# Moving operands of the matmuls to one offset modulo 256 bytes, and the wide products in order of width

## The chip, the core and the metric

The kernel runs on one core of a Trainium2 chip. The metric is the device time of one execution in microseconds. The runs below give a median; beside them stands one profiled execution, whose trace all rows are from. PE is TensorE's matmul, PEld its weight load, DVE is VectorE, ACT ScalarE, POOL GpSimd, SP SyncE.

## The reference

Two blocks of a network over 256 positions of width 1024, one after the other. All weights are float32. Reduced to what the products look like:

```
x = x + even_mixer(rmsnorm(x))          # gated convolutions, then @ w_out
x = x + conv_glu_ffn(rmsnorm(x))        # (silu(conv(h @ w_gate)) * (h @ w_up)) @ w_down
x = x + odd_mixer(rmsnorm(x))           # linear recurrence and dilated attention
x = x + conv_glu_ffn(rmsnorm(x))
for l in (0, 1):                        # second block, each norm with shift and scale
    x = x + 0.5 * g1 * swiglu(h)        # D_FF = 2816
    x = x + g2 * (pool and latent attention)(h)
    x = x + 0.5 * g3 * swiglu(h)
return rms_norm(x)
```

So there are six feed-forward networks (FFN), each 1024 to 2816 (twice) and back to 1024. They hold most of the products.

## The kernel before

Everything is kept with the channel on the partitions: X is 8 tiles of 128 channels by 256 positions. A float32 product is made of three float32r products (the rounded part `h` and the rest `l` of each factor: wh·HH, wh·HL, wl·HH). Weights arrive in 253 units of up to 1024 KB, in a fixed order. For each unit SyncE loads it into one of three `raw` buffers, ScalarE copies it to `wh` (`hi`, L1041), VectorE writes `wl = raw - wh` (`lo`, L1479), and TensorE consumes both. Each of `raw`, `wh`, `wl` has three buffers; ScalarE waits for the end of the unit that last used the buffer (`w_used`), TensorE for `split_done`.

An FFN has 11 blocks of 256 hidden channels (NFB). The first two blocks' gate and up units are **raw units** (`raw_unit`, L635): they work on the rows XH, XL before the norm's factor is known; XH is a view of FX with rows of XROW = 288 floats, of which 258 are read where the norm has a shift, else 256. The other nine blocks have two **wide units** (`paired`, L678): for each of the 8 tiles k two products of `wh` with HP[:, k] (HH and HL side by side, 512 columns, L684) into two banks, and two of `wl` with HH[:, k] (256 columns, L687). Each block ends in a **down** unit (L763 to L778): 48 products of 256 columns (L772), whose moving operands are the gated inputs, FP[0] and FP[1] by turns (views of FX, which is free by then), F0 for the first block. The mixers' products are made by `product` (L665, its matmul on L674), with HP as the moving operand, or with FX in the latent attention's q projection, or with the weights moving and HP stationary where the result is wanted by position.

The tensors lie one after another in SBUF in the order of their declarations (L327 to L364). HP, FX, XL and F0 have their own tensors of SKEW = 28 floats (112 bytes), the data, and 4 floats. `raw`, `wh`, `wl`, `ada`, X before them are multiples of 256 bytes long, HP's tensor is 16512 bytes long, T, Z and WK are multiples of 256, FX's tensor is 9344, XL's 8320, F0's 4224.

VectorE and ScalarE also do the gate's arithmetic of each block (add PSUM to the parts kept, taps of the convolution in the two FFNs of the first block, silu, product, split into FP). In five of the FFNs VectorE sums up to four 128x1024 products per block for the modulation (`ada`, L1578). The order on each engine is the order in the program text.

Of the kernel before, what the change touches and what calls it, by code (L numbers as in the profile page):

```python
# [17 lines left out]
F32R = mybir.dt.float32r  # L18
# [6 lines left out]
P = 128  # L25
D = 1024
S = 256
KD = D // P
# [2 lines left out]
NFB = F // FB  # L31
EPS = 1e-6
RW = S + 2
XROW = 288
SKEW = 28
NB = S // P

# [279 lines left out]
def build(nc, A, const, out):  # L317

    ctx = ExitStack()
    with ctx:  # L320
        def sb(name, shape, dt=F32):
            return ctx.enter_context(nc.sbuf_tensor(name, shape, dt))
# [12 lines left out]
        T = sb("T", [P, KD, S])  # L335
        Z = sb("Z", [P, 6720])
        WK = sb("WK", [P, 4608])
        FX = sb("FX", [P, SKEW + KD * XROW + 4], F32R)[:, SKEW:SKEW + KD * XROW]
        XH = FX.rearrange("p (k s) -> p k s", s=XROW)[:, :, 0:RW]
        XL = sb("XL", [P, SKEW + KD * S + 4], F32R)[:, SKEW:SKEW + KD * S].rearrange("p (k s) -> p k s", s=S)  # L340
        FP = [FX[:, 4 * XROW:4 * XROW + 1024], FX[:, 0:1024]]
        FH = [f[:, 0:512].rearrange("p (k s) -> p k s", s=S) for f in FP]
        FL = [f[:, 512:1024].rearrange("p (k s) -> p k s", s=S) for f in FP]
        F0 = sb("F0", [P, SKEW + 1024 + 4], F32R)[:, SKEW:SKEW + 1024].rearrange("p (b k s) -> p b k s", k=2, s=S)
        TF = F0[:, 0], F0[:, 1]
        G0 = sb("G0", [P, KD])
        SH = sb("SH", [P, 6, KD, 2], F32R)
# [18 lines left out]
        def bank(i, a=0, n=512, rows=slice(0, P)):  # L366
            return PS[rows, i, a:a + n]
# [15 lines left out]
        def pairs(ap, w=S):  # L383
            return ap.rearrange("p (t s) -> p t s", s=w)
# [246 lines left out]
        def _(pe):  # L631
# [3 lines left out]
            def raw_unit(n, dst, shift, first=None, between=None, narrow=P):  # L635
# [20 lines left out]
                for part in parts:  # L656
                    for m in range(2):
                        for k in part:
                            if first and m == 0 and k % 2 == 0:
                                pe.wait_ge(lr_ready, v + k // 2 + 1)  # L660
                            last = mm(bank(dst + m, 0, S, slice(0, rows[m])), lhsT=w(0, k, m * P, rows[m]), rhs=XL[:, k, :],  # L661
                                      start=False, stop=k == KD - 1, skip_group_check=True)
# [15 lines left out]
            def paired(bk, lhs, k_tiles, whole=None):  # L678

                for k in range(k_tiles):  # L680
                    if whole and k % 2 == 0:
                        pe.wait_ge(h_ready, FILL[whole] + k // 2 + 1)
                    for m in range(2):
                        mm(pairs(bank(bk + m)), lhsT=lhs(0, k, m * P), rhs=HP[:, k], start=k == 0, stop=False,  # L684
                           skip_group_check=True)
                    for m in range(2):
                        last = mm(bank(bk + m, 0, S), lhsT=lhs(1, k, m * P), rhs=HH[:, k, :], start=False,  # L687
                                  stop=k == k_tiles - 1, skip_group_check=True)
                return last
# [65 lines left out]
            def ffn(f, name):  # L755
# [3 lines left out]
                def wide(n, bk, off=0, whole=None):  # L759
                    w = weights(n, KD, off)  # L760
                    paired(bk, lambda p, k, a: w(p, k, a, P), KD, whole=whole).then_inc(w_used, 1)
# [707 lines left out]
        def _(dve):  # L1469
# [20 lines left out]
            def raw_lo(name, c, gain):  # L1490
# [6 lines left out]
                for t in (2 * c, 2 * c + 1):  # L1497
                    last = stt(XL[:, t, :], X[:, t, :], gain(t), XH[:, t, 0:S].bitcast(F32), ALU.mult, ALU.subtract)  # L1498
                last.then_inc(lr_ready, 1)
# [653 lines left out]
```

## Time and profile before

| | us |
|---|---|
| median of 3 runs | 1557.11 (1554.96 to 1557.14) |
| the profiled execution's own time | 1556.0 |
| its span, first to last instruction | 1554.1 |
| PE busy | 1529.1 (98%) |
| VectorE busy | 1254.7 (81%) |
| ScalarE busy | 848.0 (55%) |

Busy time of an engine is the time in which at least one of its instructions is under way. Matmuls overlap each other, so the mean duration of one is its latency and not what it costs; the distance from one start to the next is. The mean granted clock of TensorE over the span is 0.997 of the full one.

### The profile page before, as it was taken

The numbers are of one execution on the slowest core, as the hardware profiler recorded it, in microseconds if no ns is written. First come the engines' busy times: TensorE is split into PE (matmuls) and PEld (weight loads), VectorE is DVE, ScalarE is ACT, GpSimd is POOL, SyncE is SP. The second block draws the span as 40 slices with busy tenths as digits, with TensorE's granted clock in tenths as the row PEclk, the third lists the DMA queues.
The fourth block names the chain that finished last, engine by engine and source line by source line (L and its number), as shares of the span: only waits on it lengthen the run. The fifth ranks groups of instructions, "written<-read, shape, count | busy, mean of one in ns | idle before, by whom it ended". The sixth has DMA issues, their size and how long they took to land.

```text
span 1554.1 us, 26739 instructions
## 1 busy us (share of the span) xinstructions
PE 1529.1 (98%) x10894; PEld 1420.1 (91%) x10894; DVE 1254.7 (81%) x1588; ACT 848.0 (55%) x1014; POOL 52.0 (3%) x61
## 2 busy tenths in 40 slices
PE   9989999999999999999999999999999999999998
PEld 7989999998799999999999999999999999999997
DVE  7978989787578998978878797887888888785555
ACT  6656555564466545744446664445644456664443
POOL 1001000000010000000000010000000000100000
PEclk9999999999999999999999999999999999999999
DMA  7505886544247875498863359886598844355551
GB/s 300 204 16 193 323 317 242 193 163 160 75 138 296 308 289 190 168 338 312 317 234 140 116 195 325 319 310 230 191 331 308 313 176 166 136 191 189 188 189 68
DMA packets 59805, 344.11 MB, mean 221 GB/s; under 512 B 6800, under 2 KB 7312, under 8 KB 28752
## 3 DMA queue, kind: packets, MB, share of 16 engines
q1 hardware_dynamic: 58752, 340.80, 61.4%
q0 software_dynamic: 544, 1.97, 0.3%
q8 instruction: 54, 0.88, 0.2%
q10 hardware_dynamic: 432, 0.27, 0.1%
q14 instruction: 23, 0.19, 0.0%
HBM read 341.96 MB, written 1.05 MB: 221 GB/s over the span
## 4 chain that ended last, share of the span: by engine, by line
PE 83%; DVE 11%; ACT 3%; issue 3%; DMA 1%; SPq 0%; ACTq 0%; DVEq 0%
PE PS L684 25%; PE PS L772 23%; PE PS L687 13%; PE PS L674 7%; PE PS L652 5%; PE PS L741 3%; DVE wl L1479 3%; PE PS L661 2%; DVE Z L1822 2%; DVE XL L1498 2%; PE PS L823 1%; DMA raw<-weights 1%; ACT wh L1041 1%; DVE RS L1511 1%; PE PS L848 1%
## 5 line engine op out<-in xcount | busy, mean ns | idle before, releaser
L1479 DVE TENSOR_TENSOR wl<-raw,wh 128x2048 fp32r<-128x2048 f32 (+2 forms) x256 | 569.8, 2229 | 126.3 <-ACT wh L1041 124.5
L1041 ACT ACTIVATE wh<-raw 128x2048 fp32r<-128x2048 f32 (+2 forms) x256 | 475.7, 1860 | 125.5 <-PE PS L772 103.9
L684 PE MATMUL PS<-HP,wh 128*128 128x512 f32 x1728 | 538.6, 393 | 0.0
L687 PEld LDWEIGHTS PS<-HP,wl 128*128 128x128 f32 x1728 | 324.0, 187 | 74.4
L687 PE MATMUL PS<-HP,wl 128*128 128x256 f32 x1728 | 344.0, 281 | 0.0
L772 PE MATMUL PS<-FX,wh 128*128 128x256 f32 x1920 | 306.7, 279 | 0.0
L684 PEld LDWEIGHTS PS<-HP,wh 128*128 128x128 f32 x1728 | 265.2, 189 | 0.0
L772 PEld LDWEIGHTS PS<-FX,wh 128*128 128x128 f32 x1920 | 262.5, 188 | 0.2
L772 PE MATMUL PS<-FX,wl 128*128 128x256 f32 x960 | 197.9, 279 | 0.0
L1578 DVE SCALAR_TENSOR_TENSOR ada<-ada,AR 128x1024 f32<-128x1024 f32 x144 | 172.9, 1219 | 0.0
L772 PEld LDWEIGHTS PS<-FX,wl 128*128 128x128 f32 x960 | 149.9, 188 | 0.0
L652 PE MATMUL PS<-FX,wh 128*128 128x258 f32 (+2 forms) x592 | 143.1, 284 | 6.8 <-ACT wh L1193 1.9
L652 PE MATMUL PS<-FX,wl 128*128 128x258 f32 (+2 forms) x592 | 141.7, 282 | 0.5 <-DVE wl L1740 0.5
L1105 ACT ACTIVATE WK<-PS 128x512 f32<-128x512 f32 x54 | 32.3, 598 | 179.7 <-PE PS L687 179.7
L674 PE MATMUL PS<-HP,wh 128*128 128x256 f32 x696 | 122.1, 279 | 1.7 <-ACT HP L1072 0.9
L652 PEld LDWEIGHTS PS<-FX,wh 128*128 128x128 f32 (+1 forms) x592 | 109.9, 187 | 9.9 <-ACT FX L1056 2.7
L674 PEld LDWEIGHTS PS<-HP,wh 128*128 128x128 f32 x696 | 105.2, 188 | 7.0 <-issue 4.1
L652 PEld LDWEIGHTS PS<-FX,wl 128*128 128x128 f32 (+1 forms) x592 | 110.4, 188 | 0.7 <-DVE wl L1740 0.7
L674 PE MATMUL PS<-HP,wl 128*128 128x256 f32 x348 | 94.9, 276 | 0.0
L1134 ACT ACTIVATE WK<-PS 128x512 f32<-128x512 f32 x54 | 32.0, 592 | 97.1 <-PE PS L687 97.1
L661 PE MATMUL PS<-XL,wh 128*128 128x256 f32 (+1 forms) x592 | 76.3, 281 | 0.0
L661 PEld LDWEIGHTS PS<-XL,wh 128*128 128x128 f32 (+1 forms) x592 | 71.9, 187 | 0.5
(272 smaller groups left out, 1664.8 us busy)
## 6 DMA issues: line engine op xcount, KB each, us to landing
raw<-weights SPq DMA_DIRECT2D x242, 1024.0 KB, 5.0
ada<-ada_w SPq DMA_DIRECT2D x144, 512.0 KB, 6.5
raw<-weights SPq DMA_DIRECT2D x6, 768.0 KB, 4.4
raw<-weights SPq DMA_DIRECT2D x4, 576.0 KB, 4.7
X<-x SPq DMA_DIRECT2D x2, 512.0 KB, 5.7
raw<-weights SPq DMA_DIRECT2D x2, 512.0 KB, 6.8
out<-Z SPq DMA_DIRECT2D x4, 256.0 KB, 2.3
AR<-c POOLq DMA_DIRECT2D x1, 512.0 KB, 7.1
```

Source lines behind the costliest of these rows:

```text
L652: mm(bank(dst + m, 0, width, slice(0, rows[m])), lhsT=w(a, k, m * P, rows[m]), rhs=XH[:, k, 0:width], start=k == 0 and a == 0, stop=False, ...
L661: last = mm(bank(dst + m, 0, S, slice(0, rows[m])), lhsT=w(0, k, m * P, rows[m]), rhs=XL[:, k, :], start=False, stop=k == KD - 1, skip_gro ...
L674: last = mm(dst, lhsT=lhs(a, k), rhs=rhs(b, k), start=first and i == 0, stop=first and i == len(order) - 1, skip_group_check=not first)
L684: mm(pairs(bank(bk + m)), lhsT=lhs(0, k, m * P), rhs=HP[:, k], start=k == 0, stop=False, skip_group_check=True)
L687: last = mm(bank(bk + m, 0, S), lhsT=lhs(1, k, m * P), rhs=HH[:, k, :], start=False, stop=k == k_tiles - 1, skip_group_check=True)
L741: last = mm(bank(bk, m * S, S), lhsT=w(a, k, m * P, P), rhs=H[b][:, k, :], start=m == 0 and k == 0 and i == 0, stop=False, skip_group_chec ...
L772: last = mm(bank(m // 2, (m % 2) * S, S), lhsT=w(a, k, m * P, P), rhs=rhs(b, k), start=begins and i == 0 and m % 2 == 0, stop=False, skip_ ...
L1041: last = A_(dst(wh), src, ACT.Copy)
L1105: A_(pairs(E), PS[:, 4:6, S:], ACT.Copy).then_inc(g_copy, 1)
L1134: A_(pairs(G), PS[:, 6:8, S:], ACT.Copy).then_inc(u_copy, 1)
L1479: last = tt(dst(wl), src, dst(wh).bitcast(F32), ALU.subtract)
L1578: stt(w, w, 1.0, AR[:], ALU.mult, ALU.mult, accum_out=AS[:, bass.ds(off * KD + step, 1)]).then_inc(ada_sum, 1)
```

## The change

All moving operands except HP go into one tensor MV, which starts where FX's tensor started, 32 + 28 floats ahead of its first data. Rows of FX get 320 floats (1280 bytes, five times 256) in place of 288 (1152 bytes, four and a half times), XL and F0 follow directly. The moving data of FX (each row), FP[0], FP[1], XL and F0 then start 112 bytes past a multiple of 256, as HP does. What lies behind (G0, SH, AR, PR, CN and the rest) moves by 896 bytes. In `paired` the loop over k is split in two: all sixteen products of 512 columns, then all sixteen of 256. The number and shapes of the instructions, the semaphores and the order of units are the same.

```diff
@@ -31,7 +31,7 @@
 NFB = F // FB
 EPS = 1e-6
 RW = S + 2
-XROW = 288
+XROW = 320
 SKEW = 28
 NB = S // P
 
@@ -335,13 +335,14 @@
         T = sb("T", [P, KD, S])
         Z = sb("Z", [P, 6720])
         WK = sb("WK", [P, 4608])
-        FX = sb("FX", [P, SKEW + KD * XROW + 4], F32R)[:, SKEW:SKEW + KD * XROW]
+        MV = sb("MV", [P, 32 + SKEW + KD * XROW + KD * S + 1024 + 4], F32R)[:, 32 + SKEW:]
+        FX = MV[:, 0:KD * XROW]
         XH = FX.rearrange("p (k s) -> p k s", s=XROW)[:, :, 0:RW]
-        XL = sb("XL", [P, SKEW + KD * S + 4], F32R)[:, SKEW:SKEW + KD * S].rearrange("p (k s) -> p k s", s=S)
+        XL = MV[:, KD * XROW:KD * XROW + KD * S].rearrange("p (k s) -> p k s", s=S)
         FP = [FX[:, 4 * XROW:4 * XROW + 1024], FX[:, 0:1024]]
         FH = [f[:, 0:512].rearrange("p (k s) -> p k s", s=S) for f in FP]
         FL = [f[:, 512:1024].rearrange("p (k s) -> p k s", s=S) for f in FP]
-        F0 = sb("F0", [P, SKEW + 1024 + 4], F32R)[:, SKEW:SKEW + 1024].rearrange("p (b k s) -> p b k s", k=2, s=S)
+        F0 = MV[:, KD * (XROW + S):KD * (XROW + S) + 1024].rearrange("p (b k s) -> p b k s", k=2, s=S)
         TF = F0[:, 0], F0[:, 1]
         G0 = sb("G0", [P, KD])
         SH = sb("SH", [P, 6, KD, 2], F32R)
@@ -683,6 +684,7 @@
                     for m in range(2):
                         mm(pairs(bank(bk + m)), lhsT=lhs(0, k, m * P), rhs=HP[:, k], start=k == 0, stop=False,
                            skip_group_check=True)
+                for k in range(k_tiles):
                     for m in range(2):
                         last = mm(bank(bk + m, 0, S), lhsT=lhs(1, k, m * P), rhs=HH[:, k, :], start=False,
                                   stop=k == k_tiles - 1, skip_group_check=True)
```

## Rows read from the trace of the kernel before

**Rows 1.** The page, sections 1 and 2: busy time; 40 slices of the granted clock.

```profile
PE 1529.1 (98%) x10894; PEld 1420.1 (91%) x10894; DVE 1254.7 (81%) x1588; ACT 848.0 (55%) x1014; POOL 52.0 (3%) x61
...
PEclk9999999999999999999999999999999999999999
```

**Rows 2.** The page, section 4: the chain that ended last, by engine.

```profile
PE 83%; DVE 11%; ACT 3%; issue 3%; DMA 1%; SPq 0%; ACTq 0%; DVEq 0%
```

**Rows 3.** TensorE by line and shape: busy us, mean ns, idle us before.

```profile
L684 PE MATMUL PS<-HP,wh 128*128 128x512 f32 x1728 | 538.6, 393 | 0.0
L687 PE MATMUL PS<-HP,wl 128*128 128x256 f32 x1728 | 344.0, 281 | 0.0
L772 PE MATMUL PS<-FX,wh 128*128 128x256 f32 x1920 | 306.7, 279 | 0.0
...
L652 PE MATMUL PS<-FX,wh 128*128 128x258 f32 x336 | 82.4, 285 | 3.4 <-DVE BI L1599 1.9 <-ACT FX L1056 1.4
```

**Rows 4.** The chain in order of time: start us, us, what.

```profile
115.96 5.45 PE PS L674 x48
...
140.43 4.03 PE PS L652 x32
144.46 1.81 PE PS L661 x16
146.27 5.63 PE PS L772 x48
163.06 5.62 PE PS L772 x48
...
383.62 5.96 PE PS L674 x48
...
459.92 1.86 PE PS L661 x16
```

**Rows 5.** Timeline of PE, q projection, moving operand FX (neighbours merged).

```profile
852.40 0.28 PE L674 MATMUL PS<-FX,wl 128*128 128x256 f32 x1
...
856.98 0.28 PE L674 MATMUL PS<-FX,wl 128*128 128x256 f32 x1
```

**Rows 6.** Timeline of PE, a mixer projection, moving operand HP.

```profile
350.42 0.28 PE L674 MATMUL PS<-HP,wl 128*128 128x256 f32 x1
...
351.48 0.28 PE L674 MATMUL PS<-HP,wl 128*128 128x256 f32 x1
...
355.56 0.28 PE L674 MATMUL PS<-HP,wl 128*128 128x256 f32 x1
```

**Rows 7.** Timeline of PE in a wide unit: each k is one pair of each.

```profile
152.42 0.63 PE L684 MATMUL PS<-HP,wh 128*128 128x512 f32 x2
...
152.89 0.39 PE L687 MATMUL PS<-HP,wl 128*128 128x256 f32 x2
...
153.12 0.62 PE L684 MATMUL PS<-HP,wh 128*128 128x512 f32 x2
...
153.57 0.41 PE L687 MATMUL PS<-HP,wl 128*128 128x256 f32 x2
...
155.91 0.40 PE L684 MATMUL PS<-HP,wh 128*128 128x512 f32 x1
```

**Rows 8.** Timeline of PE, v projection: 512 columns of the weights move.

```profile
863.85 0.62 PE L674 MATMUL PS<-wh,HP 128*128 128x512 f32 x2
...
865.95 0.39 PE L674 MATMUL PS<-wh,HP 128*128 128x512 f32 x1
```

**Rows 9.** Timeline of DVE in the first FFN.

```profile
145.62 1.47 DVE L1524 TENSOR_TENSOR HP<-T,HP 128x512 fp32r<-128x512 f32 x2
...
248.80 2.29 DVE L1479 TENSOR_TENSOR wl<-raw,wh 128x2048 fp32r<-128x2048 f32 x1
...
265.86 2.29 DVE L1479 TENSOR_TENSOR wl<-raw,wh 128x2048 fp32r<-128x2048 f32 x1
```

**Rows 10.** Timeline of PE: wide units of the first FFN start.

```profile
252.41 0.62 PE L684 MATMUL PS<-HP,wh 128*128 128x512 f32 x2
...
269.19 0.39 PE L684 MATMUL PS<-HP,wh 128*128 128x512 f32 x1
```

## Prediction, on record before the changed kernel ran

> **What bounds the kernel now.** I read the page first. TensorE is busy for 1529.1 us of a span of 1554.1, at the full granted clock (2.4 GHz) in all slices [rows 1], and the chain that ended last runs over TensorE for 83% of the span and over VectorE for 11% [rows 2]. So only two things can shorten this kernel much: fewer nanoseconds per product, or fewer waits at the stage borders. The change adds and removes no instruction; it can only act on the first.
>
> Then I grouped TensorE's work by line and shape [rows 3]: 1728 products with 512 columns (L684) and 1728 with 256 (L687) in the wide units, 1920 + 960 + 288 = 3168 with 256 columns in the down products (L772, the 288 from F0), 704 raw products with 258 columns (L652: twice the 336 of the row, and 32 narrow ones) and by the code 480 with 256, 592 on XL (L661). The "mean ns" there is a latency; products overlap. What counts is the pitch, from one start to the next, which I take from the chain of waits, whose merged pieces cover back-to-back products, and from the timeline.
>
> The chain gives: a down, 48 products in 5.62 us, 117.1 ns each; 48 products of L674, which read HP, in 5.45 us, 113.5 each; 32 raw products in 4.03 us, 120 each without the 0.2 us pause at their start; 16 on XL in 1.81 us, 113.1 each, at another place in 1.86, 116 each [rows 4]. Same columns, same clock, 4 to 7 ns apart.
>
> **Why they differ, as the trace has it.** The clean comparison is one line of code with two moving operands. L674 on FX: from 852.40 to 856.98 there are 13 rounds of three products, 4.58/39 = 117.4 ns [rows 5]. L674 on HP: 350.42 to 351.48 is nine products, 117.8 ns; from 351.48 to 355.56 36 products, 113.3 ns [rows 6]. The HP run starts unevenly and after some ten products falls into step at 113.3 and stays there; the FX run never does. From the sizes in the code (tensors laid one after another) HP and XL start 112 bytes past a multiple of 256, as do odd rows of FX; even rows of FX, both FP buffers and F0 start 240 past, because WK ends on a half multiple and XROW = 288 floats is 4.5 times 256 bytes. Weights (wh, wl) start on multiples. Every group at 112 falls into step, every group at 240 does not, and no other difference runs through all of them. That the two reads of TensorE (weights for the next product, moving rows for this one) get in each other's way by their distance is my inference; the numbers need only the two pitches.
>
> **The placement, priced.**
> - Down products: 3168 go from 240 to 112. If they fall into step: 117.1 − 113.3 = 3.8 ns, so −12.0 us. They stand behind at least sixteen 256-column products on HP of the wide unit, so the uneven start is mostly spent by then. Bounds: 0 (they never fall in) and −12.0.
> - Raw products: 480 with 256 columns at about 118 go to 113.3, −2.3 us; 704 with 258 columns at 120 have no row in step; between 113.3 and 120, I take 115 (two columns more are 0.8 ns, the rest is caution), −3.5. The XL products that follow and are not in step today (116) fall in too: 592 × 2.7 ns is 1.6 at most, taken as −1.2. The q products on FX, 108, −0.4. Together −7.4. The first unit of each chain ends in waits for rows, norm and splits, which take such a gain back: three quarters count, −5.4. Bounds 0 and −8.
>
> **The order in the wide units, priced.** Now each k issues two 512s and two 256s: 0.70 us per k, 3.49 us for five k. The pairs of 256s last 0.23 and 0.24 us, 117.5 ns a product; that leaves (698 − 235)/2 = 231.5 for a 512 [rows 7]. They are never in step for long, since each pair of 512s disturbs it. Afterwards sixteen 512s, then sixteen 256s, with the same counts.
> - The 256s: behind 512s the L687 pieces last 0.40 and 0.41 us, less one latency of 0.28 [rows 3] 0.12 and 0.13, so they begin out of step; the known uneven start [rows 6] needs some ten products, from a lucky place none. I take six of sixteen at 118.5, ten at 113.3: 115.3 against 117.5, −2.2 × 1728 = −3.8 us. Bounds −7.3 (in step at once) and +1 (never).
> - The 512s: the nearest row for long runs is the v projection, with 512 columns moving from wh: 863.85 to 865.95, nine products, 233 ns [rows 8]; its operands lie the other way round, though. I take 232.2 for the run, between that and the 231.5 of now and nearer to the wide units' own: +0.7 × 1728 = +1.2 us. Bounds: −9.5 (all at 226, which is twice 113 and half of the fastest pair, 0.45 us) and +6.0 (all at 235, half of the slowest pair, 0.47 us).
> - The first wide unit of an FFN waits for HL by pairs of k, and the new order reaches the last pair sooner: twelve 512s take 2.8 us where six k took 4.2. HL is written by 147.1 [rows 9], the down in front of the unit starts at 146.27 [rows 4] and lasts 5.6, so the unit starts at 151.9: over 4 us to spare, cost nothing. Both halves of the weights were already awaited together at the unit's start, the buffer is freed at the unit's end as before, and banks 4 to 7 are handed on at the same points. The DMA queue gets its tokens from VectorE's splits, unchanged.
>
> **What is late next.** In the two conv FFNs VectorE is nearly the bound. Its split of the weights of a wide unit ends at 251.09 (248.80 + 2.29) for a unit that starts at 252.41, the next at 268.15 for 269.19 [rows 9, 10]: it has a period of 17.06 us where TensorE has 16.78, and the reserve falls by 0.28 per block, from 1.32 to 1.04, through the six blocks that also hold the ada sums. With TensorE 0.23 us faster per block (48 × 3.8 ns and 32 × 2.2, less 32 × 0.7: 0.18 + 0.07 − 0.02), plus some 0.5 us that the raw units bring forward, the sixth block has 1.04 − 1.4 − 0.5: TensorE waits 0.9 us. Two such FFNs and the uneven starts behind such a wait: +2.0 us.
>
> The Trainium skill speaks against all of this. TensorE: Matmul & The Clock Gate, Part 2, has two independent SBUF read ports on TensorE, so that loading the next tile's weights takes no bandwidth from the running matmul; by it alone placement changes nothing and the sum would be 0. The same page's back-to-back gap, N/2.4 + 2.5 ns, would be 109 and 216 here, an estimate that no pitch in [rows 4, 7] comes down to, and the two pitches of one line in [rows 5, 6] disagree with the rule, so the rows decide.
>
> **Sum.** −12.0 − 5.4 − 3.8 + 1.2 + 2.0 = −18.0 us. The profiled execution took 1556.0, two beyond its span; the median of the runs is 1557.1 with a spread of 2.2. So 1538 for a profiled one and 1539.1 for the median.
>
> **Rivals.**
> - *The 512s fall in step too*, at about 226: −9.5 in place of +1.2, so 1528.4. For it: the pair of 0.45 us at 153.12. Against: its neighbour needs 0.47, and the v projection stays at 233 over nine.
> - *The gain is given back.* The conv FFNs run at VectorE's pace and the raw stages at that of their waits; left are 44 downs of the four other FFNs, 2112 × 3.8 = 8.0, and two thirds of −3.8 + 1.2: 1547.4. For it: the falling reserve. Against: over the whole run L684 and L772 have no idle time before them [rows 3].
> - *Placement does nothing* (the two reads don't hinder each other, or the offset that matters is not this one): the order alone remains, −3.8 + 1.2, and with its bounds about nothing: 1554 to 1557. Against it stand [rows 5, 6].
> - *Slower: the rows come to lie badly.* If it is not the offset modulo 256 that sets the pitch but the place as a whole, the moved rows may fall into a slow cycle. The slowest 256-column piece is that of a projection with the operands the other way round: 48 products in 5.96 us, 0.1 of it a pause, 122 ns [rows 4]. Downs at 121 are +3.9 × 3168 = +12.4, less 2.6 from the order: 1567. It decides from a down pitch of 118, where the loss is as large as the gain of the order. Against it: XL and HP are far apart and both reach 113.3, so distance in the large seems free.
>
> **Chances.** Forecast 0.62, gain given back 0.15, 512s in step 0.12, placement does nothing 0.07, bad place 0.04. The likeliest case alone spans 1533 to 1545. The range runs to the neighbours on both sides, 1528 (fast 512s) to 1550 (given back, with the 258s not in step). 0.2% is 3.1 us, about what separates two medians of this kernel. Faster: 0.62 + 0.15 + 0.12 and a little of the third, 0.90; same 0.06; slower 0.04.
>
> **What would show it.** Right: a down piece of 5.44 us in the chain instead of 5.62; 113 to 115 ns on L652; in a wide unit an L684 stretch of sixteen products of 3.7 us, then sixteen of L687 in 1.85; small new waits of TensorE for splits (L1479) late in the two conv FFNs. Wrong: downs at 117 as before (the placement did not take), L684 near 226 or near 238, or waits for splits in every FFN. The weakest step is the 512s' pitch: 1 ns there is 1.7 us.

## The result, and the profile after

The changed kernel takes 1544.6 us (median of 4 runs, 1544.35 to 1545.4), the kernel before 1556.7 beside it; the ratio is 0.9926 with a 95% interval of 0.991 to 0.9941. That is 12.1 us less, where 18 were forecast; the time lies in the range of 1528 to 1550, near the upper end of what the likeliest case spans. The profiled execution took 1544.8, its span 1542.9 (1554.1 before).

The page of the changed kernel, busy times and the chain by engine:

```profile
PE 1514.0 (98%) x10892; PEld 1403.5 (91%) x10894; DVE 1254.1 (81%) x1588; ACT 848.9 (55%) x1014; POOL 53.3 (3%) x61
...
PE 61%; DVE 22%; issue 9%; ACT 6%; DMA 1%; DVEq 0%; ACTq 0%; SPq 0%
```

Set against [rows 1, 2]: TensorE has 15 us less work, the others the same, and the chain that ended last now runs over VectorE for 22% of the span where it was 11. That is a first hint of where the rest of the gain went; what it cost, the waits below and e8 measure.

The chain of the changed kernel in order of time (start us, us, what); L675 is a mixer product, L774 a down, L685 the sixteen 512s, L653 raw products with 258 columns:

```profile
115.57 5.45 PE PS L675 x48
...
382.01 5.96 PE PS L675 x48
...
648.04 3.84 PE PS L653 x32
653.75 5.44 PE PS L774 x48
659.18 3.69 PE PS L685 x16
```

A down has gone from 5.62 to 5.44 us [rows 4]; 5.44/48 is the 113.3 ns of a product in step. The mixer products on HP are as they were. The raw products stand at 3.84/32 = 120 ns, no better than before, though their rows now lie at 112 too.

Timeline of TensorE, changed kernel, one block of the first FFN (neighbours merged):

```profile
151.08 3.85 PE L685 MATMUL PS<-HP,wh 128*128 128x512 f32 x16
154.77 2.03 PE L689 MATMUL PS<-HP,wl 128*128 128x256 f32 x16
156.63 3.83 PE L685 MATMUL PS<-HP,wh 128*128 128x512 f32 x16
160.29 2.02 PE L689 MATMUL PS<-HP,wl 128*128 128x256 f32 x16
162.16 0.61 PE L774 MATMUL PS<-MV,wh 128*128 128x256 f32 x4
```

From start to start the first sixteen 512s take 3.69 us, 230.6 ns each, the sixteen 256s behind them 1.86, 116.3. Singly, the 512s go round in threes, 225, 231 and 238 ns; the 256s begin 119, 117, 119, 114, 120, 120, 115, 118, 121, 119 and only then stay at 113.3. Of the 108 runs of 256s behind 512s in this kernel, 106 need ten or eleven products to fall into step and two need 13; the down behind them starts in step. The second row of 512s is one of five in 108 that ran at 226.7 (its piece of 3.66 us contains a first one of 263; the other four stand behind a wait): a 512 can be in step as well, but here only by the accident of its start.

For the raw products, timeline of the changed kernel, 256 columns in the first FFN, then 258 in another:

```profile
127.83 0.28 PE L653 MATMUL PS<-MV,wh 128*128 128x256 f32 x1
...
131.46 0.39 PE L662 MATMUL PS<-MV,wh 128*128 128x256 f32 x2
...
636.16 0.28 PE L653 MATMUL PS<-MV,wh 128*128 128x258 f32 x1
...
640.00 2.02 PE L662 MATMUL PS<-MV,wh 128*128 128x256 f32 x16
```

32 products in 3.63 us, 113.4 ns, with 256 columns; 32 in 3.84, 120 ns, with 258. Same line, same rows, two columns apart.

Waits of TensorE in the changed kernel (us in total, times, longest), the first two and the new one, which comes at 251, 268, 571, 588 and 605 us, late in the two conv FFNs, where it was forecast:

```profile
PE PS L882 <- DVE Z L1849: 3.4, 2, 2.6
PE PS L653 <- ACT wh L1195: 2.4, 1, 2.4
...
PE PS L685 <- DVE wl L1481: 1.6, 5, 0.5
```

Summed from start to start over each group, with pauses apart (work and pauses in us; the pitch in ns is the mean without pauses). A pause counts with the product in front of it, so a wide unit's wait for a split stands with the down before it:

| group | pitch | work | pauses |
|---|---|---|---|
| 3168 down products | 117.07 to 113.39 | −11.7 | 0.5 to 3.4 |
| 1728 wide, 512 columns | 231.3 to 230.6 | −1.1 | 0 to 0.5 |
| 1728 wide, 256 columns | 117.5 to 116.4 | −2.0 | 0 |
| 480 raw, 256 columns | 117.7 to 114.2 | −1.7 | 2.3 to 4.1 |
| 704 raw, 258 columns | 119.9 to 119.4 | −0.3 | 2.8 to 2.8 |
| 592 on XL | 115.6 to 115.35 | −0.1 | 6.3 to 7.2 |
| 1296 of `product`, 256 columns (mixers, 108 for q, 144 with the weights moving) | 115.0 to 114.6 | −0.5 | 7.5 to 8.2 |

Together −17.4 of work and +6.9 of pauses; the other 0.7 of the span's 11.2 lies in smaller groups.

### The profile page after: what moved, and what is told of

It reads as the page before. It is cut to its first block, busy times and chain, and to the rows that moved or that the text cites. A ratio compares the mean times of both kernels' runs of the same rounds, so it can differ in the third digit from the quotient of the medians.

```text
span 1542.9 us, 26737 instructions
## 1 busy us (share of the span) xinstructions
PE 1514.0 (98%) x10892; PEld 1403.5 (91%) x10894; DVE 1254.1 (81%) x1588; ACT 848.9 (55%) x1014; POOL 53.3 (3%) x61
## 4 chain that ended last, share of the span: by engine, by line
PE 61%; DVE 22%; issue 9%; ACT 6%; DMA 1%; DVEq 0%; ACTq 0%; SPq 0%
PE PS L685 18%; PE PS L774 16%; PE PS L689 9%; DVE wl L1481 7%; PE PS L675 7%; PE PS L743 3%; DVE ada L1580 3%; ACT wh L1043 3%; PE PS L653 2%; DVE MV L1500 2%; DVE Z L1824 2%; PE PS L825 1%; DMA raw<-weights 1%; DVE RS L1513 1%; PE PS L662 1%
## 5 line engine op out<-in xcount | busy, mean ns | idle before, releaser
L1481 DVE TENSOR_TENSOR wl<-raw,wh 128x2048 fp32r<-128x2048 f32 (+2 forms) x256 | 569.8, 2229 | 119.0 <-ACT wh L1043 117.3
L685 PE MATMUL PS<-HP,wh 128*128 128x512 f32 x1728 | 416.5, 392 | 1.6 <-DVE wl L1481 1.6
L685 PEld LDWEIGHTS PS<-HP,wh 128*128 128x128 f32 x1728 | 315.9, 187 | 67.5 <-DVE wl L1481 1.9
L774 PE MATMUL PS<-MV,wh 128*128 128x256 f32 x2112 | 328.7, 275 | 0.2
L774 PEld LDWEIGHTS PS<-MV,wh 128*128 128x128 f32 x2112 | 282.2, 188 | 0.7 <-issue 0.7
L689 PE MATMUL PS<-HP,wl 128*128 128x256 f32 x1728 | 218.6, 278 | 0.0
L774 PE MATMUL PS<-MV,wl 128*128 128x256 f32 x1056 | 212.9, 275 | 0.0
L774 PEld LDWEIGHTS PS<-MV,wl 128*128 128x128 f32 x1056 | 162.5, 188 | 0.0
L653 PE MATMUL PS<-MV,wh 128*128 128x258 f32 (+2 forms) x592 | 142.2, 284 | 8.0 <-ACT wh L1195 2.4
L653 PE MATMUL PS<-MV,wl 128*128 128x258 f32 (+2 forms) x592 | 140.7, 282 | 0.5 <-DVE wl L1742 0.5
L675 PE MATMUL PS<-HP,wh 128*128 128x256 f32 x696 | 122.2, 279 | 1.9 <-ACT HP L1074 0.9
L653 PEld LDWEIGHTS PS<-MV,wh 128*128 128x128 f32 (+1 forms) x592 | 110.7, 189 | 11.3 <-ACT MV L1058 3.0
L675 PEld LDWEIGHTS PS<-HP,wh 128*128 128x128 f32 x696 | 105.3, 188 | 7.7 <-issue 4.3
L653 PEld LDWEIGHTS PS<-MV,wl 128*128 128x128 f32 (+1 forms) x592 | 110.8, 189 | 0.7 <-DVE wl L1742 0.7
L675 PE MATMUL PS<-HP,wl 128*128 128x256 f32 x348 | 94.9, 276 | 0.0
L662 PEld LDWEIGHTS PS<-MV,wh 128*128 128x128 f32 (+1 forms) x592 | 71.9, 187 | 0.5
```

What stands on the lines that cost most here:

```text
L653: mm(bank(dst + m, 0, width, slice(0, rows[m])), lhsT=w(a, k, m * P, rows[m]), rhs=XH[:, k, 0:width], start=k == 0 and a == 0, stop=False, ...
L675: last = mm(dst, lhsT=lhs(a, k), rhs=rhs(b, k), start=first and i == 0, stop=first and i == len(order) - 1, skip_group_check=not first)
L774: last = mm(bank(m // 2, (m % 2) * S, S), lhsT=w(a, k, m * P, P), rhs=rhs(b, k), start=begins and i == 0 and m % 2 == 0, stop=False, skip_ ...
L1481: last = tt(dst(wl), src, dst(wh).bitcast(F32), ALU.subtract)
```

## The experiments

The kernel before ran beside each group of experiments, at 1555.3 to 1557.1. e1, e4, e7 and e8 are medians of four executions, e2 of eight; e3, e5, e6 and e9 to e12 ran once each, so what they say rests on pitches and on differences of several us.

**The placement alone** (e1): the changed kernel with the old order.

```diff
-                for k in range(k_tiles):
                     for m in range(2):
                         last = mm(bank(bk + m, 0, S), lhsT=lhs(1, k, m * P), rhs=HH[:, k, :], start=False,
```

> The placement alone; the wide units keep two 512s and two 256s per k. Theory (placement does nearly all): downs go from 117.1 to 113.5 ns as in the changed kernel, wide units stay at 698 ns per k, the time is 1546 to 1548, some 2 above the changed kernel. Rival (the sixteen 256s ahead of a down are what brings it into step; from a mixed unit it enters out of step at each down): a down of about 5.49 us instead of 5.44, twelve uneven products, 1550.

Measured: 1549.1 us, ratio 0.9956 (0.9939 to 0.9972). The chain, downs:

```profile
145.60 5.44 PE PS L773 x48
162.21 5.49 PE PS L773 x48
178.87 5.49 PE PS L773 x48
```

The down behind raw products is in step at once, those behind mixed wide units enter out of step (120, 119, 117, 118 and so on for eleven products): 5.49 us, as the rival said, and the time lies between the two forecasts. Placement alone is worth 7.0 us.

**The order alone** (e2): the kernel before, with the loop over k split.

> The order alone; FX and F0 stay 240 bytes past the weights. Theory: downs stay at 117 ns; the 256s of the wide units gain 1.1 ns and the 512s 0.6, about 3 us together, 1553 to 1555. Rival (order helps the downs also): downs below 116, under 1550.

Measured: 1551.8 us, ratio 0.9971 (0.9961 to 0.9982). The chain:

```profile
146.49 5.63 PE PS L773 x48
152.12 3.69 PE PS L684 x16
157.62 3.69 PE PS L684 x16
163.18 5.62 PE PS L773 x48
```

Downs stay at 117.2, so the placement is what moves them. The order is worth 4.3 us, more than the 3 expected, and the time is 1.2 below the expected range: the first wide unit behind a down at 117 starts at another point of the round of the 512s, and its 256s are in step from the first in 53 of 54 cases (113.4 ns, the second unit's 116.35, 114.9 on average). 7.0 + 4.3 = 11.3 is nearly the whole of 12.1, but the parts don't simply add up. In the changed kernel the 256s keep less of the order's gain (116.4 ns where e2 has 114.9), and the downs gain by it instead (113.4 where e1 has 114.3, 2.9 us).

**All of MV at 240** (e3): the changed kernel, 32 floats further.

```diff
-        MV = sb("MV", [P, 32 + SKEW + KD * XROW + KD * S + 1024 + 4], F32R)[:, 32 + SKEW:]
+        MV = sb("MV", [P, 64 + SKEW + KD * XROW + KD * S + 1024 + 4], F32R)[:, 64 + SKEW:]
```

> The changed kernel with 32 floats more ahead of MV's data, so that all its rows lie 240 bytes past the weights modulo 256; MV stays one tensor, XROW 320, all else but the place of what follows as changed. Theory (the offset modulo 256 sets the pitch): downs and 256-column raw products at 117, XL at 117 too, no step, 1555 to 1558. Rival (the common tensor, the row length or the place in the large did it): downs stay at 113.5, 1545.

Measured: 1551.3 us, below the 1555 to 1558 expected. The chain:

```profile
115.74 5.45 PE PS L675 x48
146.09 5.62 PE PS L774 x48
```

Downs 5.62, mixers on HP (still at 112) 5.45; XL, at 240 for the first time, goes from 115.4 to 117.2. One tensor, rows of 320 floats and the order don't bring a down into step; the offset does. The time is that of e2, which it repeats in effect; my 1555 had forgotten the order's share.

**The weights moved instead** (e5), and **everything moved** (e6). In e5 the moving operands stay; in e6 only the first pad is there, so that all distances stay.

```diff
+        sb("pad0", [P, 32])
         wh = sb("wh", [P, SPL, UNIT], F32R)
         wl = sb("wl", [P, SPL, UNIT], F32R)
+        sb("pad1", [P, 32])
```

> The changed kernel with wh and wl moved on by 128 bytes and 128 more behind them, so that the moving operands stay where they are modulo 256 and lie 112 - 128, that is 240 modulo 256, past the weights. Theory (the distance between weights and moving rows sets the step): nothing is in step any more, downs and 256-column raw products at 117.2, mixer products on HP at 117 too, 1560 to 1565. Rival (the absolute place of the moving rows counts): pitches as in the changed kernel, 1545.

> The changed kernel with everything from wh on moved by 128 bytes, distances unchanged. Theory (distance): downs stay at 113.4, 1543 to 1546. Rival (absolute place): downs at 117, 1560 or more.

Measured: e5 1563.0 us, e6 1545.3. The chain of e5:

```profile
114.65 5.64 PE PS L677 x48
145.17 5.62 PE PS L776 x48
150.79 3.79 PE PS L687 x16
```

And of e6:

```profile
115.91 5.45 PE PS L676 x48
...
279.57 5.44 PE PS L775 x48
285.01 3.69 PE PS L686 x16
```

With no moving operand touched, mixers (5.45 to 5.64) and downs (5.44 to 5.62) fall out of step, and the 512s go from 230.6 to 235. With all moved alike, nothing changes. It is the distance between weights and moving rows that counts, not where either lies. This is the sharpest of the experiments. That 256 bytes is the period shows, as far as three places can, in the changed kernel: its rows of FX are 1280 bytes apart and so lie at two places by turns modulo 512, yet 32 products over all eight of them take 113.4 ns each, while 112 and 240, 128 apart, differ.

**258 or 256 columns** (e7): all raw products have 256 columns; the two columns of the shift are left out.

```diff
-                width = RW if shift else S
+                width = S
```

> The changed kernel whose raw products all have 256 columns: the two columns of the shift are left out, so the shift's share in the raw units is missing. Theory (the 258 columns are what keeps these 704 products out of step, and a good part of the rest is given back to waits in front of the FFNs): L653 at 113.3 everywhere, 704 x 6 = 4.2 us and 0.8 at the XL products less new waits of about half, 1541 to 1543. Rival (all of it is lost in waits): pitch at 113.3, time 1544 to 1545. Rival (258 is not the cause): 119 as before, 1544.

Measured: 1543.6 us, ratio 0.9919 (0.9902 to 0.9936), 1.0 less than the changed kernel (1543.2 to 1544.0 against 1544.35 to 1545.4), between the theory's 1541 to 1543 and the 1544 to 1545 of the rival in which waits take all. The pitch on L653 is 114.1 over all 1184 products, so the two columns are what keeps 704 of them out of step. From start to start the raw products take 4.8 us less, and 1.4 us of span remain: the pauses behind the XL products, most of them in front of the next raw unit, rise by 1.7, and those behind the mixer products by 1.2.

**Less work for VectorE in the conv FFNs** (e8): the ada sums there run over half of the columns, the other half is left out.

```diff
-                            ada_step(ADA_AT[FFNS[f]], off, k)
+                            ada_step(ADA_AT[FFNS[f]], off, k, D // 2 if conv else D)
```

> The changed kernel whose ada sums in the two conv FFNs run over half of the columns (the other half is left out), about 0.5 us less of VectorE's time for each of 48, 2 us per block. Theory (VectorE's splits hold TensorE up late in these two FFNs): the waits on L1481 go, some 2.5 us, 1542. Rival (these waits cost nothing in the end, or are DMA's or ScalarE's): 1544.5.

Measured: 1542.3 us, ratio 0.991 (0.9893 to 0.9926), 2.3 less than the changed kernel, 1542.0 to 1542.4 against 1544.35 to 1545.4. The wide units no longer wait for L1481, the pauses at downs fall from 3.4 to 1.1 us, the pitches of downs, 512s and 256s are the same within 0.15 ns. So about 2.3 us of the gain are given back to VectorE's splits in two FFNs, where 2.0 were forecast.

**Wide units of 256-column products alone** (e4): each 512 is cut in two, HH and HL, with the weights loaded for each. The three products of a k and m then follow each other, for all k.

```diff
-                        mm(pairs(bank(bk + m)), lhsT=lhs(0, k, m * P), rhs=HP[:, k], start=k == 0, stop=False,
-                           skip_group_check=True)
-                for k in range(k_tiles):
-                    for m in range(2):
+                        for b in range(2):
+                            mm(bank(bk + m, b * S, S), lhsT=lhs(0, k, m * P), rhs=HP[:, k, b], start=k == 0 and b == 0,
+                               stop=False, skip_group_check=True)
```

> The changed kernel with each 512-column product of the wide units cut in two of 256 columns (HH, then HL, same weights, loaded twice), 1728 products more. Theory (256-column products on an operand at 112 stay in step at 113.3, and a 512 costs 230.6, more than two of those): a wide unit takes 48 x 113.3 = 5.44 us instead of 5.55, 108 units give 12 us, less 2 to 4 given back to waits for splits: 1534 to 1537. Rival (TensorE cannot keep up with a third more loads, or HL behind HH breaks the step): 48 at 117, 5.62 us, 1552.

Measured: 1536.6 us, ratio 0.9876 (0.986 to 0.9893): 8 us below the changed kernel, with 1728 products and weight loads more (half more in the wide units, 16% over the kernel). TensorE's groups:

```profile
L686 PE MATMUL PS<-HP,wh 128*128 128x256 f32 x3456 | 591.9, 275 | 3.3 <-DVE wl L1480 3.3
L688 PE MATMUL PS<-HP,wl 128*128 128x256 f32 x1728 | 475.4, 275 | 0.0
```

And its timeline, from the start of two wide units to the down behind them:

```profile
658.88 0.39 PE L686 MATMUL PS<-HP,wh 128*128 128x256 f32 x2
...
669.76 0.61 PE L773 MATMUL PS<-MV,wh 128*128 128x256 f32 x4
```

96 products in 10.88 us, 113.3 ns each, against 11.10 for the same work in the changed kernel. Two 256s in step take 226.7 ns, less than one 512 out of step, and behind them the next product is in step. Over 54 such pairs of units that is some 12 us. The time fell by 8: the pauses at downs and in the wide units grow by 3.1 us (waits for splits 3.3 us where they were 1.6, and the restart behind each).

**Other distances** (e9 to e12), on e4, with HP and MV each at a distance of its own.

> The kernel of 256-column wide units (e4) with two other offsets past the weights modulo 256: HP at 48 and MV at 176. Theory A (steps exist only in a narrow band of offsets near 112): HP out of step, wide products and mixers at 116 or more, MV also, 117; some 25 us above e4, 1560. Theory B (a band half of 256 wide round 112, say 48 to 176, is all good): both at 113.3, 1537. Theory C (only 240 and its neighbours are bad): as B.

> The same kernel (e4) with HP at 144 and MV at 80 past the weights modulo 256, 32 bytes to either side of 112. Theory A (narrow band): at least one of the two groups is out of step, its products at 115 to 118: 1545 to 1560. Theories B and C (wide band): both at 113.3, 1537.

> The kernel e4 with HP at 128 and MV at 96 past the weights modulo 256, 16 bytes to either side of 112. After e9 and e10 (48, 80 and 176 at 118 to 120, 144 at 115) the good offsets are a band between 80 and 144. If it is as wide as 32 bytes, both are in step at 113.3: 1537. If only the side towards 144 is good, HP is in step and MV is not: downs at 117 to 119, 1550 to 1555. If 112 alone is good, both are out: 1560.

> The same with HP at 120 and MV at 104, 8 bytes to either side of 112. A band of 16 bytes or more: both in step, 1537. If 112 alone is good: 1550 to 1560.

Measured, one execution each: 1576.7, 1561.0, 1580.4 and 1602.3 us. The chain of e12, a mixer product on HP and a down:

```profile
114.79 5.88 PE PS L675 x48
146.22 5.76 PE PS L773 x48
```

Mean pitch of 256-column products by distance past the weights modulo 256, pauses left out (HP: the wide units, or mixers for 240; MV: the downs):

| bytes | 48 | 80 | 96 | 104 | 112 | 120 | 128 | 144 | 176 | 240 |
|---|---|---|---|---|---|---|---|---|---|---|
| ns | 118.3 | 119.7 | 119.9 | 120.1 | 113.4 | 122.2 | 118.7 | 115.0 | 119.2 | 117.2 |

The 115.0 at 144 is a mean of two levels. The chain of e10, three downs; between them stand 96 products of two wide units each:

```profile
164.00 5.75 PE PS L773 x48
...
181.14 5.75 PE PS L773 x48
...
197.78 5.75 PE PS L773 x48
```

From the end of the first down to the second the wide units take 11.39 us, 118.6 ns a product; from the end of the second to the third 10.89, 113.4. So it is in all of e10: 38 of the 54 pairs of wide units run at 113.4, the other 16 at 118.6 to 118.8, and none changes on its way. Two stretches of mixer products are in step, one of them only behind a short pause in its middle; the others lie between 116.6 and 119.9. At 144 the step exists, but a stretch that starts out of it doesn't fall in by itself. At 112 it does, within ten or so products, and that holds for 112 alone of the ten distances tried; at the remaining eight no wide unit, mixer or down settles at 113.3. 8 bytes to either side of 112 cost 7 to 9 ns. My picture of a band was wrong. Theory A of e9 was right for its two distances, but all four times came out above what the narrow band was given (1560, 1545 to 1560, 1560, 1550 to 1560). Against e4 the worst pair of distances costs 66 us, four per cent of the kernel, with not one instruction changed.

## Why the forecast was right, and where it was off

- **Placement of the downs**: −12.0 forecast, −11.7 measured, by the mechanism named: e3, e5 and e6 leave only the distance between weights and moving rows.
- **Raw, XL and q products**: −7.4 before waits, −2.5 measured (−2.1 without q). This is the term that was mis-sized. I had no row of 258 columns in step and took 115 ns; it is 119.4, and e7 shows that the two extra columns are the reason. With them the uneven start of the XL products stays, too. The 120 ns that the prediction starts from was misread: the 32 products in 4.03 us [rows 4] belong to the first FFN, which has 256 columns, and the piece runs to the end of the last one; from start to start they take 3.87 us, 117.6 ns without the pause. That products of 258 columns stood at 119.9 was luck. The upper end of the range allowed for this miss ("with the 258s not in step").
- **256s of the wide units**: six uneven products of sixteen assumed, ten or eleven measured: −2.0 in place of −3.8, well inside its bounds.
- **512s**: +1.2 forecast, −1.1 measured, an error that hid part of the others. The v projection, with its operands the other way round, was a poor stand-in; the wide units' own mean of 231 was the better one.
- **Given back**: +2.0 for VectorE's reserve in the conv FFNs; e8 measures 2.3, at the place forecast. The quarter of the raw gain that I wrote off was too little: all pauses together grew by 6.9, of which 2.9 stand at downs and 3.5 on raw, XL and mixer products. e7 shows the same on its own: 4.8 us less work, 1.0 us less time.

So the work came out at −17.4 for −22.0 (the terms before waits), and the waits at +6.9 for +4.0. The mechanism of the largest term was right and is shown; that the total still fell in the range owes something to the width of the range. The rival that would have made the 512s fast was half seen, in single units after a pause. The one in which the rows come to lie badly did not come true here, and e9 to e12 show that it was no idle one: seven of the eight distances besides 112 and 240 give a worse mean than 240. What decides there is still the distance modulo 256, not, as that rival had it, the place as a whole.

What is not settled is why 112. The experiments vary the distance and find the step; that it comes from two reads hindering each other remains an inference. Open too is what makes some starts bring the 512s, or the stretches at 144, into step and others not.

## What to carry to other kernels

Where TensorE streams float32r operands back to back, take the start-to-start distance of equal products from the timeline and compare tensors: a few ns between two operands on one line of code is a matter of placement, and it is worth trying distances in single steps, since the only reliably good one here was one of ten. Try products of equal width: here a run of one width in step cost less than a mix with fewer, wider products, even with half more weight loads in those units (10.88 against 11.10 us). And when TensorE is at 98%, look first at how much reserve the engine that feeds it has, since 6.9 of 17.4 us went there and into the stage borders.

## What the runs showed of the hardware that was not expected

A 256-column product costs 113.3 ns in step and up to 122 out of it, at the same granted clock (0.997 to 0.999 of 2.4 GHz over every profiled span), by the distance modulo 256 bytes between its weights and its moving rows. At 144 bytes both levels occur in one run, 113.4 and 118.7, by how a stretch starts (e10). The Trainium skill (TensorE: Matmul & The Clock Gate, Part 2) gives TensorE two independent read ports, so that loading weights takes no read bandwidth from the running product. This kind of stream does not behave as if the two were independent: with the weights alone moved by 128 bytes (e5) the time goes from 1544.6 to 1563.0, with weights and rows moved together (e6) it stays at 1545.3. A product of 258 columns costs 119.4 at the distance at which one of 256 costs 113.4. And a 512-column product, 230.6, costs more than two of 256 in step with a weight load each, 226.7.
